# The first MLP's up-projection: 15 of its 22 pairs of output tiles by seven products instead of eight

## The chip, the cores and the metric

One core of one Trainium2 chip runs the whole program. The metric is the device time of one execution in microseconds (us); lower is better. TensorE (PE) does the matmuls, ScalarE (ACT), VectorE (DVE) and GpSimd (POOL) work on 128 x n tiles in SBUF and PSUM, and SyncE (SP) issues the DMA transfers. Each of these engines runs its own instructions strictly in the order of the program, and they wait for each other with counting semaphores.

## What is computed

Three layers on x of 512 rows (sequence) by 1024 columns in float32. The first layer has gated linear attention beside sliding-window attention, and then the gated MLP that the change is about; two more layers (dilated and differential attention, each with a squared-relu MLP) follow.

```python
h2 = rms_norm(x, ffn_norm)                       # 512 x 1024
u = causal_dwconv(h2 @ w_up, conv_w, conv_b)     # w_up 1024 x 5632, 3 taps along the sequence
a, bval = jnp.split(u, 2, axis=-1)               # 2 x 2816 columns
x = x + (jax.nn.silu(a) * bval) @ w_down         # w_down 2816 x 1024
```

## The kernel before

Everything is kept transposed: 128 features on the partitions, the 512 positions of the sequence along the free axis. Each float32 operand is split into a high part, rounded to `fp32r`, and a low part, the rest; a product is high x high + high x low + low x high, accumulated in PSUM.

**The up-projection.** w_up has 44 tiles of 128 output columns. They are taken in 22 pairs, one tile of `a` and the tile of `bval` that it gates; pair i gives block i of the gated result. `up_tile` is one tile: 8 blocks of the inner dimension, 24 matmuls of 512 columns (lines 1033, 1034, 1038), so a pair is 48. The weights come from HBM into the two halves of `stage`; ACT rounds a tile to `w_hi` (`split_hi`, line 1506), POOL makes `w_lo` in four pieces of 256 columns (`split_lo`, line 507). Four PSUM banks (`UP`) hold two pairs.

**Behind a tile** stands a fixed sequence: DVE scales the bank by `rstd` (line 2445), ACT begins the convolution (line 1767), DVE adds the other two taps (lines 2447 and 2450). Behind a pair: ACT silu (line 1770), DVE multiplies the halves (line 2455), ACT rounds the block to `f1_hi` (line 1772), DVE makes `f1_lo` (line 2458). All this is a hardware loop that does two pairs in one pass.

**The down-projection** follows: for each of the 8 output tiles, 22 blocks f times three matmuls of 512 columns (lines 1080, 1081, 1086). The order of all work is written out by hand for each engine.

**Seven products** are used already in the down-projections of the two later MLPs (`product`, lines 1425 to 1455, `fast_down`). The 2 x 2 block product of weights A and activations B is done in the Winograd form, with 7 products of half size: A11, S1, A12, S2, S4, S3, A22, where S1 to S4 are sums of blocks of A. A product is 12 matmuls of 256 columns (lines 1444, 1445, 1453). A group of four weight blocks is a quad; `slot_hi` and `slot_lo` hold its split blocks, `SUM_X` and `SUM_Y` are PSUM banks in which sums are made. In those MLPs DVE adds each product straight into x in SBUF (line 2890).

## Time and profile before

| | |
|---|---|
| device time, median of 3 runs | 1718.95 us (1718.62 to 1719.03) |
| the profiled execution | 1718.6 us, of which the span of the core's work is 1716.8 us |
| TensorE's granted clock | 0.999 of 2.4 GHz |
| busy: PE, DVE, ACT, POOL | 99%, 62%, 51%, 56% of the span |
| instructions in the trace | 27243, of which 9425 matmuls |

The profile is of one execution; times of single instructions and gaps come from it. Busy shares are averages over stages with different limits.

### The profile page before, as it was taken

The page shows a single profiled execution, that of the slowest core. Times are in us where ns is not written, and L with a number is a line of the kernel's source. Part 1 is how long each engine was busy: PE and PEld are TensorE (multiplying, and loading weights), DVE is VectorE, ACT ScalarE, POOL GpSimd, SP SyncE. Part 2 cuts the span into 40 slices and gives each one's busy share as a digit, 9 for nine tenths or more (in the row PEclk, how much of TensorE's full clock was granted, in tenths as well). Part 3 has the DMA queues.
Part 4 walks back from the last instruction along what each step waited for, and adds up shares of the span by engine and source line. Part 5 has one row for each costly group of instructions (what it writes and reads, how often), then busy time and mean ns, then how long its engine had stood idle before and what let it go on. Part 6 is the DMA issues. An engine that isn't in the chain of part 4 may idle for free.

```text
span 1716.8 us, 27243 instructions
## 1 busy us (share of the span) xinstructions
PE 1704.7 (99%) x9425; PEld 1440.6 (84%) x9425; DVE 1061.0 (62%) x2084; ACT 868.3 (51%) x1498; POOL 963.1 (56%) x1095
## 2 busy tenths in 40 slices
PE   9999999999999999999999999999999999999998
PEld 7778888888888778888989898977777889898988
DVE  6875755555311455568757575867776676757576
ACT  5665555555322444435545444546655554545355
POOL 5543655555555434357666666755554665656666
PEclk9999999999999999999999999999999999999999
DMA  5221333332334322223323323233322242333332
GB/s 192 74 68 61 100 98 98 97 93 93 108 95 137 104 68 83 74 74 123 99 98 99 105 96 106 64 128 116 105 97 70 87 133 91 109 99 98 99 98 74
DMA packets 48662, 167.91 MB, mean 98 GB/s; under 512 B 5376, under 2 KB 6672, under 8 KB 48528
## 3 DMA queue, kind: packets, MB, share of 16 engines
q1 hardware_dynamic: 48272, 166.05, 30.2%
q8 instruction: 61, 1.00, 0.2%
q10 hardware_dynamic: 288, 0.52, 0.1%
q14 instruction: 41, 0.34, 0.1%
HBM read 164.31 MB, written 2.24 MB: 97 GB/s over the span
## 4 chain that ended last, share of the span: by engine, by line
PE 90%; DVE 6%; ACT 2%; issue 1%; DMA 0%; POOL 0%; SPq 0%; DVEq 0%; ACTq 0%
PE bank L736 18%; PE bank L1444 6%; PE bank L1453 6%; PE bank L1445 6%; PE bank L661 5%; PE bank L660 5%; PE bank L666 5%; PE bank L1033 5%; PE bank L1034 5%; PE bank L1038 5%; PE bank L754 3%; PE bank L760 3%; PE bank L755 3%; PE bank L1086 2%; PE bank L1081 2%; PE bank L1080 2%
## 5 line engine op out<-in xcount | busy, mean ns | idle before, releaser
L507 POOL TENSOR_TENSOR w_lo<-stage,w_hi 128x256 fp32r<-128x256 f32 x872 | 672.2, 803 | 571.7 <-ACT w_hi L1506 317.5
L1506 ACT ACTIVATE w_hi<-stage 128x1024 fp32r<-128x1024 f32 x218 | 229.4, 1052 | 200.9 <-PE bank L1081 54.7
L660 PE MATMUL bank<-xn_hi,w_hi 128*128 128x512 f32 x544 | 211.8, 389 | 0.0
L661 PE MATMUL bank<-xn_lo,w_hi 128*128 128x512 f32 x544 | 211.7, 389 | 0.0
L736 PE MATMUL bank<-xn_hi,w_hi 128*128 128x512 f32 x464 | 189.1, 407 | 0.0
L736 PE MATMUL bank<-xn_lo,w_hi 128*128 128x512 f32 x464 | 181.8, 392 | 0.0
L2890 DVE TENSOR_TENSOR x<-x,bank 128x256 f32<-128x256 f32 (+1 forms) x217 | 97.4, 455 | 89.3 <-PE bank L1453 86.6
L1453 PE MATMUL bank<-arena 128*128 128x256 f32 x896 | 146.6, 283 | 0.0
L1033 PE MATMUL bank<-xn_hi,w_hi 128*128 128x512 f32 x352 | 137.1, 389 | 0.0
L1034 PE MATMUL bank<-xn_lo,w_hi 128*128 128x512 f32 x352 | 136.9, 389 | 0.0
L666 PE MATMUL bank<-xn_hi,w_lo 128*128 128x512 f32 x544 | 135.0, 389 | 0.0
L1444 PE MATMUL bank<-arena 128*128 128x256 f32 x512 | 129.4, 284 | 1.3 <-DVE arena L2910 0.8
L1445 PE MATMUL bank<-arena 128*128 128x256 f32 x512 | 128.7, 283 | 0.0
L1453 PEld LDWEIGHTS bank<-arena 128*128 128x128 f32 x896 | 124.8, 192 | 0.0
L736 PE MATMUL bank<-xn_hi,w_lo 128*128 128x512 f32 x464 | 123.9, 399 | 0.0
L666 PEld LDWEIGHTS bank<-xn_hi,w_lo 128*128 128x128 f32 x544 | 102.1, 188 | 21.2
L661 PEld LDWEIGHTS bank<-xn_lo,w_hi 128*128 128x128 f32 x544 | 102.2, 188 | 21.1
L660 PEld LDWEIGHTS bank<-xn_hi,w_hi 128*128 128x128 f32 x544 | 102.1, 188 | 20.9
L2910 DVE TENSOR_TENSOR arena<-tmp,arena 128x256 fp32r<-128x256 f32 (+2 forms) x128 | 115.0, 917 | 3.8 <-ACT arena L2067 2.5
L736 PEld LDWEIGHTS bank<-xn_hi,w_hi 128*128 128x128 f32 x464 | 87.2, 188 | 25.2 <-issue 8.5
L736 PEld LDWEIGHTS bank<-xn_hi,w_lo 128*128 128x128 f32 x464 | 84.6, 188 | 22.8 <-issue 6.0
L736 PEld LDWEIGHTS bank<-xn_lo,w_hi 128*128 128x128 f32 x464 | 87.3, 188 | 16.0
(374 smaller groups left out, 3719.3 us busy)
## 6 DMA issues: line engine op xcount, KB each, us to landing
stage<-weights SPq DMA_DIRECT2D x219, 512.0 KB, 3.6
prob<-pairs SPq DMA_DIRECT2D x32, 512.0 KB, 3.6
stage<-pairs SPq DMA_DIRECT2D x32, 512.0 KB, 3.6
bias<-table SPq DMA_DIRECT2D x11, 896.0 KB, 6.4
out<-y SPq DMA_DIRECT2D x8, 256.0 KB, 2.2
x<-x_in SPq DMA_DIRECT2D x3, 512.0 KB, 7.6
bias<-swa_table SPq DMA_DIRECT2D x4, 256.0 KB, 4.4
con<-consts SPq DMA_DIRECT2D x1, 640.0 KB, 9.8
```

The costliest lines, as they stand in the source:

```text
L507: ins = nc.gpsimd.tensor_tensor(w_lo[:, p_, ks], stage[:, p_, ks], w_hi[:, p_, ks].bitcast(F32), ALU.subtract)
L660: pe.matmul(G[p_][:], w_hi[:, p_, k], hi[:, k], start=(first and k == ks[0]), stop=False)
L661: mm = pe.matmul(G[p_][:], w_hi[:, p_, k], lo[:, k], start=False, stop=False)
L666: mm = pe.matmul(G[p_][:], w_lo[:, p_, k], hi[:, k], start=False, stop=(last and k == ks[-1]))
L736: mm = pe.matmul(G[p_][:], (w_hi if i < 2 * KD else w_lo)[:, p_, k], (xn_lo if i < 2 * KD and i % 2 else xn_hi)[:, k], start=(i == 0), sto ...
L1033: pe.matmul(UP[bank][:], w_hi[:, p_, k], xn_hi[:, k], start=(k == 0), stop=False)
L1034: mm = pe.matmul(UP[bank][:], w_hi[:, p_, k], xn_lo[:, k], start=False, stop=False)
L1444: pe.matmul(region, w, fc_hi[:, i, f], start=(fresh and i == 0), stop=False, skip_group_check=True)
L1445: pe.matmul(region, w, fc_lo[:, i, f], start=False, stop=False, skip_group_check=True)
L1453: mm = pe.matmul(region, w, fc_hi[:, i, f], start=False, stop=(i == QUADS - 1), skip_group_check=True)
L1506: act.activation(w_hi[:, p_], stage[:, p_], ACT.Copy).then_inc(hi_ready, 1)
L2910: dve.tensor_tensor(fc_lo[:, i, a:b + 1].rearrange("p c s -> p (c s)"), src, fc_hi[:, i, a:b + 1].rearrange("p c s -> p (c s)").bitcast(F3 ...
```

## The change

The up-projection takes 7 pairs as before (`N_PLAIN`) and the other 15 (`Q_UP`) by seven products. The four blocks of a quad are now the two tiles of a pair, each cut in the two halves of the inner dimension; the factors of B are the two halves of the normalized x by the two halves of the sequence.

- **Factors of B.** During plain pairs 0 to 3 DVE, ACT and POOL make the seven factors, high and low, from x and `rstd` (`factors_first`, `factors_second`, `factor_highs`, `factor_lows`). They lie in the upper part of `arena`.
- **Weights.** A quad comes from HBM as two transfers of 512 KB, two quads ahead. ACT copies one block to PSUM (`up_copy`), DVE makes the four sums (`up_sum`), ACT rounds seven blocks (`up_high`), DVE makes two of the low parts (`up_sum_low`) and POOL five (`up_low`).
- **Results.** They can't be added into an SBUF accumulator, since the convolution needs the product of the pair alone. Of the four quarters, C_00 is P1 + P2 and so on: ACT copies the partial products P1, U2 and U3 to SBUF and P5 to the pair's bank (`p1_copied`, `u2_copied`, `u3_copied`, `p5_copied`), and DVE adds (`c_00`, `c_01`, and two adds in `c_1`). There is no scaling by `rstd` for these pairs: it is in the factors.
- **Gating.** POOL now multiplies silu(a) by bval (`f_made_of`), for all pairs. The rounding (`f_high`) and the low parts (`f_low`) are done later: blocks 0 to 7 during quads 4 to 12, into the weight buffers `w_hi` and `w_lo` that are not used there; blocks 8 to 21 at the end of the last quad and behind it.
- **Down.** The first four down tiles are split on the way from the last quad (`down_split_hi`, `down_split_lo`) into slots that come free. Output tile 0 takes all its low parts of f last.
- **No loops.** The hardware loop of the up-projection is written out in line on all engines; the order on ACT and DVE where the plain pairs end is its own.

The diff, cut to its core:

```diff
-N_UP1 = 2 * NF1
+N_PLAIN = 7
+FACTORS_AT = [0, 1, 2, 3]
+Q_UP = NF1 - N_PLAIN
+N_UP1 = 2 * N_PLAIN
+UP_ORDER = [HI_A11, HI_S1, HI_A12, HI_S2, HI_S4, HI_A22, HI_S3]
+N_EARLY = 8
+EARLY_AT = 4
...
         def _(sp):
+            def up_load(q):
+                if q == 1:
+                    sp.wait_ge(lo_ready, T_DOWN1)
+                elif q >= 2:
+                    sp.wait_ge(slot_low, UP_LOW_AT[HI_A22, q - 2])
...
+            sp.wait_ge(slot_low, UP_LOW_AT[HI_A22, Q_UP - 1 - (Q_UP % 2)])
+            loads(T_DOWN1, T_QKV[0])
...
         def _(pool):
+            for q in range(Q_UP):
+                up_low(HI_S3, q)
+                if q == 0:
+                    up_low(HI_A22, 0)
+                if q + 1 < Q_UP:
+                    up_low(HI_A11, q + 1)
+                f_made_of(N_PLAIN + q - 1)
+                if q + 1 < Q_UP:
+                    for k in (HI_A12, HI_S4, HI_A22):
+                        up_low(k, q + 1)
+            for s_ in range(3):
+                down_split_lo(T_DOWN1 + s_)
+            f_made_of(NF1 - 1)
...
         def _(pe):
+            def up_product(q, k):
+                region = R2 if k in (HI_A12, HI_A22) else R5 if k in (HI_S1, HI_S4) else R1[q % 2][:, 0:HS]
...
+                elif k == HI_S2:
+                    pe.wait_ge(up_moved, moved_at(q, P1_COPY))
+                elif k == HI_S4:
+                    pe.wait_ge(up_moved, moved_at(q, P5_COPY))
+                elif k == HI_A22:
+                    pe.wait_ge(product_added, 4 * q + C_00)
+                elif k == HI_S3:
+                    pe.wait_ge(up_moved, moved_at(q, U2_COPY))
+                for i in range(QUADS):
+                    w, cols = up_hi[k][:, i * P:(i + 1) * P], slice(i * HS, (i + 1) * HS)
+                    pe.matmul(region, w, factor[:, f, 0, cols], start=(fresh and i == 0), stop=False, skip_group_check=True)
+                    pe.matmul(region, w, factor[:, f, 1, cols], start=False, stop=False, skip_group_check=True)
...
+                        if d == 0:
+                            pe.wait_ge(ffh_ready, FFH_PREP + f + 1)
...
         def _(act):
+            def p5_copied(q):
+                act.wait_ge(product_done, N_PROD * q + UP_AT[HI_S1])
+                act.wait_ge(conv_2, 2 * (N_PLAIN + q))
...
+            def up_copy(q):
+                act.wait_ge(quad_full[q % 2], 32 * (q // 2 + 1))
+                if q:
+                    act.wait_ge(sum_made, N_SUM * q)
+                act.activation(SUM_X[:], up_raw(q, 1)[:, 0:S], ACT.Copy).then_inc(slot_high, 1)
...
+            down_split_hi(T_DOWN1 + 2)
+            u3_copied(Q_UP - 1)
+            f_high(12)
+            conv_0_of(NF1 - 1, 1)
+            f_high(13)
+            silu(NF1 - 1)
+            for f in range(14, NF1 - 1):
+                f_high(f)
+            down_split_hi(T_DOWN1 + 3)
+            f_high(NF1 - 1)
...
         def _(dve):
+            up_sum_low(0, HI_S1)
+            scaled(N_PLAIN - 1, 1)
+            conv(N_PLAIN - 2, 1)
+            up_sum_low(0, HI_S2)
+            conv(N_PLAIN - 1, 0)
+            for q in range(Q_UP):
+                i, more = N_PLAIN + q, q + 1 < Q_UP
+                if q:
+                    c_1(q - 1)
+                else:
+                    conv(i - 1, 1)
+                if more:
+                    up_sum(q + 1, HI_S1)
+                    up_sum(q + 1, HI_S3)
+                    up_sum(q + 1, HI_S2)
+                if q:
+                    conv(i - 1, 1)
+                c_00(q)
+                if more:
+                    up_sum(q + 1, HI_S4)
+                    up_sum_low(q + 1, HI_S1)
+                    up_sum_low(q + 1, HI_S2)
+                c_01(q)
...
+                conv(i, 0)
+                if EARLY_AT < q <= EARLY_AT + N_EARLY:
+                    f_low(q - EARLY_AT - 1)
```

**DVE between two pairs.** Before, this is the loop's second pair (bank3 is the tile of bval, bank2 that of a):

```order
L2445 TENSOR_TENSOR bank3<-bank3,rstd 128x512
L2446 REGISTER_ALU
L2447 ISA
L2447 SCALAR_TENSOR_TENSOR tmp<-bank3,par,tmp 128x511
L2450 ISA
L2450 SCALAR_TENSOR_TENSOR tmp<-bank3,par,tmp 128x510
L2453 REGISTER_ALU
L2455 TENSOR_TENSOR bank2<-bank2,tmp 128x512
L2458 ISA
L2458 TENSOR_TENSOR arena<-bank2,arena 128x512
L2438 REGISTER_ALU
L2438 COMPARE_AND_BRANCH
```

After, this is one quad q from 5 to 12, from its second sum to its last instruction (`f_low`, line 2931); ahead of it stand the two adds of `c_1` on bank1 (lines 2923 and 2924) and the first sum (line 2882):

```order
L2886 TENSOR_TENSOR xn_raw<-stage,bank5 128x512
L2889 TENSOR_TENSOR bank5<-bank6,stage 128x512
L2832 SCALAR_TENSOR_TENSOR tmp<-bank1,par,tmp 128x511
L2835 SCALAR_TENSOR_TENSOR tmp<-bank1,par,tmp 128x510
L2910 TENSOR_TENSOR bank0<-rstd,bank4 128x256
L2894 TENSOR_TENSOR xn_raw<-stage,bank5 128x512
L2900 TENSOR_TENSOR v_split<-bank6,v_split 128x512
L2900 TENSOR_TENSOR bias_slots<-bank5,bias_slots 128x512
L2916 TENSOR_TENSOR bank0<-rstd,bank7 128x256
L2832 SCALAR_TENSOR_TENSOR tmp<-bank0,par,tmp 128x511
L2835 SCALAR_TENSOR_TENSOR tmp<-bank0,par,tmp 128x510
L2931 TENSOR_TENSOR arena<-arena_raw,w_hi 128x512
```

Eight arithmetic instructions for a pair have become fourteen, fifteen with `f_low`; the convolution (lines 2832, 2835) now has sums, adds and low parts ahead of it and between its halves, and the loop's register instructions are gone.

**ACT between two pairs.** Before, the second pair of a pass; line 1767 is the start of the convolution, 1770 silu, 1772 the rounding of the gated block:

```order
L1764 REGISTER_ALU
L1767 ISA
L1767 ACTIVATE tmp<-bank2,par 128x512
L1770 ACTIVATE bank2<-tmp 128x512
L1506 ACTIVATE w_hi<-stage 128x1024
L1764 REGISTER_ALU
L1767 ISA
L1767 ACTIVATE tmp<-bank3,par 128x512
L1771 REGISTER_ALU
L1772 ISA
L1772 ACTIVATE arena<-bank2 128x512
L1759 REGISTER_ALU
```

After, quad 4 from the second convolution of the pair before (line 2005 on bank1) on, with its copies of P5 (line 2051) and U2 (line 2057), the highs (line 2039), the copy to PSUM (line 2026) and the rounding of block 0 (line 2072, into w_hi):

```order
L2005 ACTIVATE tmp<-bank1,par 128x512
L2039 ACTIVATE v_split<-stage 128x512
L2051 ACTIVATE bank1<-bank7 128x256
L2039 ACTIVATE v_split<-bank6 128x512
L2039 ACTIVATE bias_slots<-stage 128x512
L2057 ACTIVATE rstd<-bank2 128x256
L2039 ACTIVATE bias_slots<-bank5 128x512
L2039 ACTIVATE bias_slots<-xn_raw 128x512
L2005 ACTIVATE tmp<-bank0,par 128x512
L2039 ACTIVATE xn_hi<-stage 128x512
L2026 ACTIVATE bank5<-xn_raw 128x512
L2072 ACTIVATE w_hi<-arena_raw 128x512
```

Two roundings of 1024 columns have become seven of 512 for a pair, and four copies of 256 and one of 512 are new; the copy of P5 now stands behind the start of the convolution of the pair before (line 2005).

**ACT where the up-projection ends.** Before, from the rounding of a pair's gated block, the loop's last instruction, on:

```order
L1772 ACTIVATE arena<-bank 128x512
L1759 REGISTER_ALU
L1759 COMPARE_AND_BRANCH
L1546 ACT_TABLE_LOAD
L1506 ACTIVATE w_hi<-stage 128x1024 x2
L1782 ACTIVATE xn_hi<-x,par 128x512
L1783 ACTIVATE tmp<-x 128x512
L1506 ACTIVATE w_hi<-stage 128x1024 x3
```

After, behind the last U2 copy: the start of the last pair's first convolution, then down tile 2 (line 2081 into v_split), the U3 copy (line 2063), the end of the last pair's convolution (line 2005) and silu (line 2011), and the roundings of blocks 11 to 21 (line 2072):

```order
L2005 ACTIVATE tmp<-bank,par 128x512
L2072 ACTIVATE arena<-arena_raw 128x512
L2081 ACTIVATE v_split<-stage 128x1024
L2063 ACTIVATE xn_raw<-bank 128x256
L2072 ACTIVATE arena<-arena_raw 128x512
L2005 ACTIVATE tmp<-bank,par 128x512
L2072 ACTIVATE arena<-arena_raw 128x512
L2011 ACTIVATE tmp<-tmp 128x512
L2072 ACTIVATE arena<-arena_raw 128x512 x2
L2072 ACTIVATE arena<-xn_raw 128x512 x5
L2081 ACTIVATE bias_slots<-stage 128x1024
L2072 ACTIVATE arena<-xn_raw 128x512
```

One rounding of a gated block ahead of the down-projection has become eleven, and ten of them stand behind a split that waits for a transfer.

## Rows read from the trace of the kernel before

**Rows 1.** The page: clock granted to TensorE in the 40 slices

```profile
PEclk9999999999999999999999999999999999999999
```

**Rows 2.** Waits of PE, whole run: us in total, times, longest

```profile
PE bank L920 <- DVE arena L2175: 1.5, 1, 1.5
```

**Rows 3.** Chain that ended last, 180 to 600: start us, us, what

```profile
431.54 1.81 PE bank L1038 x8
436.98 1.81 PE bank L1038 x8
442.42 1.81 PE bank L1086 x8
```

**Rows 4.** Timeline of PE, 844 to 848: start us, us, what, count

```profile
844.32 0.64 PE L1453 MATMUL bank<-arena 128*128 128x256 f32 x4
...
844.80 0.28 PE L1444 MATMUL bank<-arena 128*128 128x256 f32 x1
...
846.24 0.28 PE L1444 MATMUL bank<-arena 128*128 128x256 f32 x1
```

**Rows 5.** Timeline of ACT, 838 to 846; idle before in brackets

```profile
837.87 0.63 ACT L2031 ACTIVATE arena<-stage 128x512 fp32r<-128x512 f32 x1
...
838.39 0.60 ACT L2020 ACTIVATE bank<-prob 128x512 f32<-128x512 f32 x1
...
842.47 0.60 ACT L2031 ACTIVATE v_split<-bank 128x512 fp32r<-128x512 f32 x1 [2.60 <-DVE bank L2837]
...
842.96 0.62 ACT L2031 ACTIVATE v_split<-prob 128x512 fp32r<-128x512 f32 x1
...
845.06 0.63 ACT L2031 ACTIVATE arena<-v_tok 128x512 fp32r<-128x512 f32 x1 [0.84 <-PE bank L1453]
```

**Rows 6.** Timeline of DVE, 840 to 846

```profile
841.02 0.68 DVE L2834 TENSOR_TENSOR qkv<-prob,bank 128x512 f32<-128x512 f32 x1
841.73 0.70 DVE L2837 TENSOR_TENSOR bank<-bank,prob 128x512 f32<-128x512 f32 x1
842.34 0.41 DVE L2890 TENSOR_TENSOR x<-x,bank 128x256 f32<-128x256 f32 x1
842.67 0.68 DVE L2842 TENSOR_TENSOR v_tok<-prob,bank 128x512 f32<-128x512 f32 x1
843.27 0.68 DVE L2848 TENSOR_TENSOR arena<-bank,v_split 128x512 fp32r<-128x512 f32 x1
```

**Rows 7.** Timeline 300 to 325 of ACT, DVE and POOL, first MLP

```profile
304.03 0.78 ACT L1767 ACTIVATE tmp<-bank,par 128x512 f32<-128x512 f32 x1 [0.71 <-DVE bank L2445]
...
304.96 0.75 DVE L2447 SCALAR_TENSOR_TENSOR tmp<-bank,par,tmp 128x511 f32<-128x511 f32 x1 [1.10 <-ACT tmp L1767]
...
305.85 0.75 DVE L2450 SCALAR_TENSOR_TENSOR tmp<-bank,par,tmp 128x510 f32<-128x510 f32 x1
...
314.56 1.06 ACT L1506 ACTIVATE w_hi<-stage 128x1024 fp32r<-128x1024 f32 x1
...
315.53 0.76 ACT L1767 ACTIVATE tmp<-bank,par 128x512 f32<-128x512 f32 x1
...
315.78 2.83 POOL L507 TENSOR_TENSOR w_lo<-stage,w_hi 128x256 fp32r<-128x256 f32 x4 [4.57 <-ACT w_hi L1506]
```

**Rows 8.** Groups by form, whole run: count | busy us, mean ns | idle before

```profile
L549 POOL TENSOR_TENSOR arena<-stage,arena 128x512 fp32r<-128x512 f32 x16 | 20.8, 1298 | 0.5
...
L2910 DVE TENSOR_TENSOR arena<-tmp,arena 128x512 fp32r<-128x512 f32 x32 | 30.5, 953 | 0.0
...
L2059 ACT ACTIVATE arena<-tmp 128x256 fp32r<-128x256 f32 x32 | 13.4, 418 | 1.0
```

**Rows 9.** Timeline 831.7 to 832.9: PE resumes behind DVE

```profile
831.75 0.96 DVE L2910 TENSOR_TENSOR arena<-tmp,arena 128x768 fp32r<-128x768 f32 x1
...
832.85 0.36 PE L1444 MATMUL bank<-arena 128*128 128x256 f32 x1 [0.29 <-DVE arena L2910]
```

**Rows 10.** The page: DMA issues, KB each, median us to landing

```profile
stage<-weights SPq DMA_DIRECT2D x219, 512.0 KB, 3.6
```

More of the change, by code:

```diff
@@ L151, in program @@
             pass
+        with nc.sbuf_tensor("xn_raw", [P, 2 * KD, S], F32) as xn_raw:
+            pass
         xn_hi = sb("xn_hi", [P, KD, S], F32R)
@@ new lines, in program, with up_raw, up_s3 @@
+        up_slots += [xn_hi[:, 0], xn_hi[:, 1]]
+        up_hi = {k: up_slots[2 * i] for i, k in enumerate(SLOT_ORDER)}
+        up_lo = {k: up_slots[2 * i + 1] for i, k in enumerate(SLOT_ORDER)}
+        def up_raw(q, r):
+            if q % 2:
+                return stage[:, r].rearrange("p k c -> p (k c)")
+            blocks = xn_raw[:, KD + 2 * r:KD + 2 * r + 2] if q else arena_raw[:, 12 + 2 * r:14 + 2 * r]
+            return blocks.rearrange("p k s -> p (k s)")
+        def up_s3(q):
+            return xn_raw[:, 3 - q % 2] if q else arena_raw[:, 10]
@@ L210, in program @@
         MB = banks[7]
-        UP = banks[0:4]
         END_MEAN = (MB, OB)
@@ new lines, in f_made_of, with f_low, down_low @@
+            def f_made_of(i):
+                pool.wait_ge(silu_done, i + 1)
+                pool.wait_ge(conv_2, 2 * i + 2)
+                nc.gpsimd.tensor_tensor(f1[i], conv_acc(i, 0), conv_acc(i, 1), ALU.mult).then_inc(f_made, 1)
+            def f_low(f):
+                pool.wait_ge(ffh_ready, FFH_PREP + f + 1)
+                nc.gpsimd.tensor_tensor(f1_lo[f], f1[f], f1_hi[f].bitcast(F32), ALU.subtract).then_inc(factor_low, 1)
+            def down_low(t):
+                for k in range(0, KD, KD // 4):
+                    ks = slice(k, k + KD // 4)
+                    ins = nc.gpsimd.tensor_tensor(down_lo(t)[:, ks], stage[:, t % 2, ks], down_hi(t)[:, ks].bitcast(F32), ALU.subtract)
+                ins.then_inc(lo_ready, 1)
@@ new lines, in _ @@
+            for s_ in range(3):
+                down_split_lo(T_DOWN1 + s_)
+            f_made_of(NF1 - 1)
+            for f in POOL_LOWS:
+                f_low(f)
+            down_split_lo(T_DOWN1 + 3)
+            with pool.Fori((T_DOWN1 + 4) // 2, T_QKV[0] // 2) as m:
+                for p_ in range(2):
+                    pool.wait_ge(hi_ready, 2 * m + p_ + 1)
+                    pool.wait_ge(tile_done, 2 * m + p_ - 1)
+                    down_low(T_DOWN1 + 4 + p_)
+            split_los(T_QKV[0], T_MLP2[0])
@@ new lines, in _ @@
+            split_hi(T_MLP1 // 2 + 1, 0)
+            for i in range(N_PLAIN - 1):
+                conv_0_of(i, 0)
+                split_hi(T_MLP1 // 2 + i + 1, 1)
+                if i == N_PLAIN - 2:
+                    act.wait_ge(tables_saved, 80)
+                    up_copy(0)
+                silu(i)
+                conv_0_of(i, 1)
+                if i < N_PLAIN - 2:
+                    split_hi(T_MLP1 // 2 + i + 2, 0)
+                if i in FACTORS_AT:
+                    factor_highs(FACTORS_AT.index(i))
@@ new lines, in _ @@
+            act.wait_ge(ff_ready, FF_PREP)
+            act.wait_ge(factor_low, QUADS)
+            up_high(HI_A11, 0)
+            up_high(HI_S1, 0)
+            up_high(HI_A12, 0)
+            conv_0_of(N_PLAIN - 1, 0)
+            up_high(HI_S2, 0)
+            up_high(HI_S4, 0)
+            up_copy(1)
+            for q in range(Q_UP):
+                i, more = N_PLAIN + q, q + 1 < Q_UP
+                if q == 0:
+                    p1_copied(0)
+                    conv_0_of(i - 1, 1)
+                    up_high(HI_S3, 0)
+                    silu(i - 1)
+                    up_high(HI_A22, 0)
+                else:
+                    u3_copied(q - 1)
+                    silu(i - 1)
+                    up_high(HI_S3, q)
+                    p1_copied(q)
+                    if not more:
+                        down_split_hi(T_DOWN1)
+                    conv_0_of(i - 1, 1)
+                if more:
+                    up_high(HI_A11, q + 1)
+                p5_copied(q)
+                if more:
+                    up_high(HI_S1, q + 1)
+                    up_high(HI_A12, q + 1)
+                else:
+                    down_split_hi(T_DOWN1 + 1)
+                    for f in range(N_EARLY, 11):
+                        f_high(f)
+                u2_copied(q)
+                if more:
+                    up_high(HI_S2, q + 1)
+                    up_high(HI_S4, q + 1)
+                conv_0_of(i, 0)
+                if more:
+                    up_high(HI_A22, q + 1)
+                else:
+                    f_high(11)
+                if q + 2 < Q_UP:
+                    up_copy(q + 2)
+                if EARLY_AT <= q < EARLY_AT + N_EARLY:
+                    f_high(q - EARLY_AT)
@@ new lines, in f_low @@
+            def f_low(f):
+                dve.wait_ge(ffh_ready, FFH_PREP + f + 1)
+                if f >= N_IN_ARENA:
+                    dve.wait_ge(product_done, N_PROD * Q_UP)
+                dve.tensor_tensor(f1_lo[f], f1[f], f1_hi[f].bitcast(F32), ALU.subtract).then_inc(ff_ready, 1)
+            for i in range(N_PLAIN - 1):
+                scaled(i, 0)
+                conv(i, 0)
+                if i - 1 in FACTORS_AT:
+                    factor_lows(FACTORS_AT.index(i - 1))
+                if i in FACTORS_AT:
+                    factors_first(FACTORS_AT.index(i))
+                scaled(i, 1)
+                if i < N_PLAIN - 2:
+                    conv(i, 1)
+                if i in FACTORS_AT:
+                    factors_second(FACTORS_AT.index(i))
@@ L2461, in _ @@
+            c_1(Q_UP - 1)
+            f_low(10)
+            conv(NF1 - 1, 1)
+            for f in DVE_LOWS:
+                if f > 10:
+                    f_low(f)
+            dve.wait_ge(f_made, NF1)
             dve.memset(acc, 0.0).then_inc(acc_zero, 1)
```

472 lines of the change are left out of this document (362 added, 110 removed).

## Prediction

> **What bounds the kernel now.** I read the clock first, then PE's waits, then the chain of work that ended last, then the timelines of the places the change touches. TensorE has its full clock, 2.4 GHz, in every slice [rows 1]. Its longest wait in the whole run is 1.5 us, and not in the first MLP [rows 2]. In the chain a tile of the up-projection starts 5.44 us after the one before, and the first down tile as long after the last up tile [rows 3]: the stage is PE's stream and nothing else, 5.44 / 24 = 0.227 us for a matmul of 512 columns, 10.88 us for a pair. So a pair is worth what its matmuls take, as long as the other engines keep up; and where they don't, the wait is new.
>
> **What is removed.** A quad has 7 x 12 = 84 matmuls of 256 columns. In the later MLPs a product takes 846.24 - 844.80 = 1.44 us, 0.12 for a matmul [rows 4], so a quad is 10.08 us. That is 0.80 us less than a pair now, for 15 pairs **12.0 us**. (Half the columns cost more than half the time, 0.120 against 0.227; with exactly half it would be 20 us.) Nothing else leaves PE's stream; down, 528 matmuls, stays.
>
> **What is added, per quad.** The prices are the distances from start to start, since the next instruction starts before the last one ends. DVE [rows 6]: 0.61 for 512 columns with one operand in PSUM, 0.33 for 256 (taken as 0.34), 0.71 where it waits for its own predecessor. ACT: 0.52 for 512 from SBUF (837.87 to 838.39), 0.49 from PSUM (842.47 to 842.96) [rows 5]. ACT's 256 from PSUM isn't in the rows: 0.418 us for 256 from SBUF [rows 8] against 0.63 for 512 is 0.21 less, so I take 0.28 to the next start and 0.39 to its end, the 512 from PSUM less that difference. Bounds: 0.25 (half of 0.49) and 0.42; two of them are in the round below. The start of a convolution is 0.78 long, the next two steps 0.75 each [rows 7]. POOL's 512 is 1.30 [rows 8]; six make 7.8 us, so POOL isn't near the limit.
> DVE in sum: four adds 1.36, four sums 2.5, two lows 1.2, two convolutions 2.9: 8.0 us of 10.08. ACT: seven highs and a copy to PSUM 4.1, four copies 1.1, two starts 1.35, silu 0.52: 7.1 us. Neither is full. But they hand work to each other, each in fixed order, and the round of these handovers is the thing to time.
>
> **The round of DVE and ACT.** Count from the first add of `c_1`. Two adds 0.68, three sums 1.93, the convolution 0.78 + 0.75 and a handover of 0.04: 4.18. Then `p5_copied` 0.28, S1 and A12 high 1.01, `u2_copied` 0.28, S2 high 0.63: 6.38. DVE's low of S2 0.61, `c_01` 0.47, ACT's start of the next convolution 0.81, DVE's two steps 0.78 + 0.67: **9.72 us**, 0.36 less than PE's 10.08. The handovers are those of the later MLPs, 0.04 (DVE at 842.43 to ACT at 842.47 [rows 5, 6]).
> In PE's time: the U3 copy starts 0.26 after the last product's end (845.06 against 844.80 [rows 4, 5]), so `c_1` at 0.69, and P5 is copied at 0.69 + 4.18 + 0.39 = 5.26. Product S4 is the fifth and wants its region at 5.76. PE needs 0.14 from DVE's end (832.71) to its own start, and loses 0.07 on the first matmul (0.36 instead of 0.28) [rows 9], so the margin is 0.29 us. This is the place where PE waits first. C_00 (5.1 against 7.2) and U2 (6.5 against 8.6) have more.
>
> **Quads 5 to 12** also have `f_low` at the end of the round, with both inputs in SBUF. Such a DVE instruction of 512 columns takes 953 ns in the mean where POOL works beside it [rows 8] against 0.68 for one with PSUM, and POOL is then in its low of A22. I take 0.95, to the next start 0.87: the round is 10.59, 0.51 over PE's. Eight times 0.51 less the margin is **3.8 us**. Bounds: alone it would be 0.61 (10.33, 1.7 us in all); behind the 0.5 us that is left of a POOL instruction 1.11 (10.83, 5.7 us). ACT's `f_high` fits.
> The Trainium skill, "SBUF — State Buffer", section "SBUF: two separate sides", says that DVE with two SBUF inputs and GpSimd exclude each other for a whole instruction. The rows agree in direction, 953 ns instead of 0.68 us. By that rule `f_low` would wait about 0.39 for the low of A22 and then take 0.69, and the sum would be some 1.0 us higher.
>
> **Where the plain pairs end** DVE is behind, since the banks of pair 6 are read only once its matmuls are done. From the start of quad 0: `scaled` to 0.81, convolution of pair 5 to 2.26, low of S2 ends 2.95; only then may ACT copy for quad 1 (`up_copy` waits for that low), then P1 (due 4.32, there at 3.9), and start the convolution of tile 13 at 3.76. DVE: tile 12 to 4.32, tile 13 from 4.57 to 6.10. ACT is then in A11 high until 6.50, P5 is copied at 6.89, S4 starts at 7.10 instead of 5.76. C_00 stands behind three sums and ends at 8.37; A22 starts at 8.58 and quad 1 at 11.46, **1.38 us** late. In quad 1 the round is still 1.18 late and margin 0.29: **0.89**. Quads 2 to 4 make it up at 0.36 each. Together 2.3 us; bounds 1.4 (quad 1 unhindered) and 3.5.
>
> **Where the quads end.** The down-projection's tile 0 needs the 22 highs in turn; block 21 is wanted behind 21 high and 16 low matmuls, 37 x 0.227 = 8.4 us after the last product. ACT comes to it late. In quad 14 a split of 0.97 stands ahead of the convolution of pair 20, which starts at 2.95 and ends at 5.3; POOL's multiplication (1.30) waits for it, so its low parts of down tile 0 run from 6.6 to 9.45 (2.83 for four pieces [rows 7]). Only then may tile 2 be loaded into the same half of `stage`; 3.6 us [rows 10] to 13.1, that is 3.0 after the last product. ACT waits for it ahead of the U3 copy. Then tile 2's split 0.97 (1.06 long, 314.56 to 315.53 [rows 7]), U3 0.28, block 12, `c_1` on DVE until 5.3, the convolution's start, block 13, silu 7.0, seven blocks 10.7, tile 3's split 11.6, block 21 at 12.3. PE restarts at 12.46 instead of 8.39: **4.1 us**. Bounds: 2.5 if the transfer takes 2 us or POOL is earlier, 5 if POOL is held up by DVE's low parts.
>
> **Moved at no cost.** The factors: in pairs 0 to 3 DVE keeps four convolution steps (3.0) and two scalings (1.4) and gets about 6 us of factors (eight instructions, by 0.34 to 0.95 each); POOL has two tiles' low parts, 5.7, plus 1.30 and, for 1024 columns of factors, 2.6. Both near 10; the cover is two pairs of PSUM banks (PE needs a bank a whole pair later), and if it failed the price would be some 0.5 us a pair, 2 us. A quad's transfers: issued 0.8 us into quad q - 2, two times 3.6 in a row end at 8.0, `up_copy` wants them at 9.4. SP has nothing else queued there.
>
> **Sum.** -12.0 + 2.3 + 3.8 + 4.1 = -1.8 us on the profiled 1718.6, which is 0.35 below the median of 1718.95. Prediction 1717.2 us.
>
> **Rivals.**
> 1. *The handovers cost what they cost in the present loop.* There ACT's end at 304.81 to DVE's start is 0.15, and a convolution step 0.89 instead of 0.78 [rows 7]. Four handovers 0.12 dearer and two steps 0.11 dearer make the round 10.42, 11.29 with `f_low`. Then quads with and without it lose 1.21 and 0.34 each: 8 x 1.21 + 6 x 0.34 = 11.7 in place of 3.8, and 0.4 more at the start: 6.5 us slower, 1725.5. For it: the same instructions. Against it: in the loop a register instruction stands ahead of each wait, and none does after. It decides the sign from 0.15 us a quad in the round on. Chance 0.18; with other new waits on this side (late POOL lows, factors) 0.23.
> 2. *Better cover.* `f_low` finds POOL idle (1.7) and the end costs 2.5: -5.5, 1713.4. Chance 0.32; the bounds of all terms together give -12.0 + 1.4 + 1.7 + 2.5 = -6.4, 1712.5.
> 3. *Full gain*, if the round is nowhere late and ACT not at the end: 1707. Against it: the end needs only rows that are there. Chance 0.02.
> Forecast as worked out, 1715.5 to 1722: 0.43.
>
> **How the numbers follow.** 0.2%, 3.4 us, is about what a measurement of this kernel can tell from no change. Faster takes rivals 2 and 3, 0.34; slower 0.22; same 0.44. The range 1711.5 to 1725 reaches past rival 2 with all its bounds and to rival 1; the dearer bound of the two copies, 0.28 in the round, is 2.2 us over quads 5 to 12 and inside it. The likeliest one's own is 1715 to 1721.
>
> **What would show it.** Product starts 1.44 apart in the quads; quad 0 about 11.5 us and quad 1 about 11.0, with PE waiting for the P5 copy (line 2051) and C_00 (line 2910); quads 2 to 4 at 10.08; quads 5 to 12 near 10.6, waiting for the P5 copy; PE waiting for line 2072 or ACT for the transfer of a down tile, some 4 us, in the first down tile; `f_low` near 0.95 us. It is wrong if a quad without `f_low` takes over 10.1, if waits show in the plain pairs, if the granted clock falls below 2.4 GHz where PE idles, or if down tile 2 is there in time.

## The result and the profile after

The changed kernel takes 1724.04 us in the median of 9 runs (1723.23 to 1724.91), the kernel before 1718.9 (1718.56 to 1719.03): a ratio of 1.003 [1.002, 1.004], 5.1 us slower. The number lies in the predicted range of 1711.5 to 1725, but the forecast was 1717.2 us and "same", so it has the sign wrong (-1.8 us forecast, +5.1 measured). The profiled executions differ by as much: spans of 1721.9 and 1716.8 us.

To see where that is, PE's stream in the first MLP is cut into three parts by the starts of its first matmuls. The first is the 14 tiles of the plain pairs, which before go at 7.01, 5.58 and then 5.44 us. The second is 15 quads, which took 15 x 10.88 = 163.2 us as pairs. The third is the first down tile of 66 matmuls, 66 x 0.227 = 14.96 us. Starts one after the other in the trace after, in us:

```
plain tiles  7.02 5.57 5.44 5.44 5.44 5.44 5.44 6.98 5.58 8.71 6.34 5.91 5.45 5.44
quads        11.51 11.15 10.08 10.08 10.08 10.08 10.34 10.59 10.59 10.60 10.58 10.61 10.58 10.58 10.33   (sum 157.78)
down tile 0  19.08
```

| part | predicted | measured |
|---|---|---|
| plain pairs | 0 | +6.3 |
| quads: matmuls saved | -12.0 | -12.0 |
| quads 0 and 1 late | +2.3 | +2.5 |
| quads made late by `f_low` | +3.8 | +4.1 |
| down tile 0 | +4.1 | +4.1 |
| sum | -1.8 | +5.0 |

Four of the five terms came out within 0.3 us of what was worked out. The one that was put at nothing cost 6.3 us.

The waits of PE after (us in total, times, longest), to be read beside [rows 2]:

```profile
PE bank L1263 <- ACT bank L2051: 4.0, 9, 1.2
PE bank L1228 <- POOL w_lo L623: 2.0, 2, 1.8
PE bank L1308 <- ACT arena L2072: 1.6, 2, 1.1
...
PE bank L1223 <- ACT w_hi L1744: 1.4, 2, 1.0
```

The wait that was longest before is no longer among the first three. L1263 is a product of a quad waiting for a region that ACT copied, L1308 the down-projection waiting for gated blocks. Both were forecast. L1228 and L1223 belong to the plain pairs: PE there waits for the halves of the weights, from POOL and from ACT, which it never did before.

**The plain pairs.** PE's timeline after, tiles 9 and 10, counted from 0 (start us, us, what, idle before in brackets):

```profile
255.55 2.66 PE L1228 MATMUL bank<-xn_hi,w_lo 128*128 128x512 f32 x8 [1.81 <-POOL w_lo L623]
258.66 0.80 PE L1223 MATMUL bank<-xn_hi,w_hi 128*128 128x512 f32 x1 [0.45 <-ACT w_hi L1744]
```

PE's idle time is put down to POOL and ACT. But both are waiting themselves, each for the next: POOL for ACT's high half, ACT for DVE. The same time on POOL, ACT and DVE, from their timelines:

```profile
244.40 3.21 POOL L623 TENSOR_TENSOR w_lo<-stage,w_hi 128x256 fp32r<-128x256 f32 x4 [3.19 <-ACT w_hi L1744]
247.56 1.29 POOL L726 TENSOR_TENSOR arena_raw<-tmp 128x512 f32<-128x512 f32 x1
248.81 2.41 POOL L712 TENSOR_TENSOR arena<-arena_raw,arena 128x1024 fp32r<-128x1024 f32 x1
```

```profile
242.60 0.78 ACT L2005 ACTIVATE tmp<-bank,par 128x512 f32<-128x512 f32 x1 [5.88 <-DVE bank L2825]
243.28 1.04 ACT L1744 ACTIVATE w_hi<-stage 128x1024 fp32r<-128x1024 f32 x1
246.34 0.42 ACT L2017 ACTIVATE arena<-arena_raw 128x256 fp32r<-128x256 f32 x1 [2.02 <-DVE arena_raw L2862]
246.66 1.47 ACT L2018 ACTIVATE arena<-arena_raw 128x1536 fp32r<-128x1536 f32 x1
248.04 0.76 ACT L2005 ACTIVATE tmp<-bank,par 128x512 f32<-128x512 f32 x1
...
256.89 0.78 ACT L2005 ACTIVATE tmp<-bank,par 128x512 f32<-128x512 f32 x1 [5.86 <-DVE bank L2825]
```

```profile
237.10 1.22 DVE L2871 TENSOR_TENSOR arena<-v_tok,arena 128x512 fp32r<-128x512 f32 x1
238.25 1.22 DVE L2851 SCALAR_TENSOR_TENSOR arena_raw<-x,par,rstd 128x512 f32<-128x512 f32 x1
239.40 1.22 DVE L2853 SCALAR_TENSOR_TENSOR arena_raw<-x,par,rstd 128x512 f32<-128x512 f32 x1
...
241.87 0.70 DVE L2825 TENSOR_TENSOR bank<-bank,rstd 128x512 f32<-128x512 f32 x1
243.41 0.75 DVE L2832 SCALAR_TENSOR_TENSOR tmp<-bank,par,tmp 128x511 f32<-128x511 f32 x1 [0.85 <-ACT tmp L2005]
...
248.83 0.75 DVE L2832 SCALAR_TENSOR_TENSOR tmp<-bank,par,tmp 128x511 f32<-128x511 f32 x1 [1.92 <-ACT tmp L2005]
...
256.15 0.70 DVE L2825 TENSOR_TENSOR bank<-bank,rstd 128x512 f32<-128x512 f32 x1
```

From the scaling (L2825) of one pair's tile to the same of the next pair is 256.15 - 241.87 = 14.28 us, and ACT's convolution starts are as far apart (256.89 - 242.60 = 14.29). PE makes a pair in 10.88. So each pair with factors falls 3.4 us further behind. In the round DVE waits 0.85 + 1.92 = 2.8 us for ACT, and has some 11.5 us of work, in which every instruction of 512 columns with its inputs in SBUF takes 1.22 us. DVE's 0.85 is ACT's own start of the convolution, 0.78 long, with the handovers. The 1.92 is an order: ACT starts the pair's second convolution (248.04) only behind the factors' highs (246.34 and 246.66), and these wait for DVE. POOL stands idle for 3.19 us of the same round; the other 11.1 us it works, longer than PE's pair as well. Its four pieces from 251.18 take 4.3 us, where four such pieces take 2.83 in [rows 7]. Neither DVE nor ACT waits for POOL in this round: it is closed by DVE and ACT alone.

**The quads.** PE's timeline after, quad 7, where it waits for the copy of P5:

```profile
358.96 0.64 PE L1271 MATMUL bank<-arena,bias_slots 128*128 128x256 f32 x4
...
360.40 0.64 PE L1271 MATMUL bank<-arena,bias_slots 128*128 128x256 f32 x4
361.33 0.35 PE L1263 MATMUL bank<-arena,bias_slots 128*128 128x256 f32 x1 [0.30 <-ACT bank L2051]
```

Products are 360.40 - 358.96 = 1.44 us apart, as in [rows 4]. The next one, due at 360.88 (360.40 + 0.48 for the four matmuls), starts at 361.33, with a first matmul of 0.35 instead of 0.28, much as in [rows 9]. DVE's timeline has the cause: `f_low` (L2931) takes 0.96 us, 0.89 to the next start, at the end of the round that leads up to this copy.

```profile
355.74 0.96 DVE L2931 TENSOR_TENSOR arena<-arena_raw,w_hi 128x512 fp32r<-128x512 f32 x1
356.63 0.42 DVE L2923 TENSOR_TENSOR bank<-xn_raw,bank 128x256 f32<-128x256 f32 x1
```

**The end.** ACT's timeline after: the split of down tile 2 waits for its transfer, then the U3 copy, and the rounding of the last of the 22 gated blocks starts 11.0 us after the last product's end (439.58) and ends 11.6 us after it.

```profile
442.10 1.06 ACT L2081 ACTIVATE v_split<-stage 128x1024 fp32r<-128x1024 f32 x1 [2.47 <-DMA stage<-weights]
443.07 0.36 ACT L2063 ACTIVATE xn_raw<-bank 128x256 f32<-128x256 f32 x1
...
450.57 0.62 ACT L2072 ACTIVATE arena<-xn_raw 128x512 fp32r<-128x512 f32 x1
```

The chain that ended last after, where [rows 3] had 1.81 us for eight matmuls, and the windows over the down tile (length, then busy us and count of PE, PEld, DVE, ACT and POOL, the granted clock as a share of 2.4 GHz, DMA share, GB/s):

```profile
447.67 2.98 PE bank L1315 x8
```

```profile
440.00:447.00 7.00, 5.40 (x22) 3.75 (x21) 5.42 (x9) 4.59 (x8) 5.96 (x8) 1.00 0.43 148
447.00:451.00 4.00, 3.97 (x12) 3.03 (x12) 4.00 (x6) 4.00 (x8) 1.66 (x2) 0.63 0.39 131
```

PE's waits are 1.6 us of the 4.1. Behind them the granted clock was 0.63 over 4 us, that is, part of that stretch ran at the lower level of 1.2 GHz, and eight matmuls took 2.98 us there. As an estimate from that row, 4 x (1 - 0.63) = 1.5 us of the 4.1 is the clock's; the last 1 us stands in neither. [rows 1] had full clock in every slice; here the dip is too short to show in a slice of 43 us.

### The profile page after: what moved, and what is told of

Same layout as the page of the kernel before. It is cut to its first block, busy times and chain, and to the rows that moved or that the text cites. A ratio compares the mean times of both kernels' runs of the same rounds, so it can differ in the third digit from the quotient of the medians.

```text
span 1721.9 us, 28210 instructions
## 1 busy us (share of the span) xinstructions
PE 1699.8 (99%) x9965; PEld 1458.2 (85%) x9965; DVE 1136.7 (66%) x2214; ACT 898.7 (52%) x1635; POOL 1023.9 (59%) x1076
## 4 chain that ended last, share of the span: by engine, by line
PE 68%; DVE 4%; ACT 1%; issue 1%; POOL 0%; DMA 0%; DVEq 0%; ACTq 0%; SPq 0%; POOLq 0%
PE bank L923 14%; PE bank L1682 6%; PE bank L1691 6%; PE bank L1683 6%; PE bank L847 6%; PE bank L848 6%; PE bank L853 6%; PE bank L1315 2%; PE bank L1308 2%; PE bank L1310 2%; PE bank L941 2%; PE bank L947 2%; PE bank L942 2%; PE bank L1541 1%; PE bank L1570 1%; DVE arena L3435 1%
## 5 line engine op out<-in xcount | busy, mean ns | idle before, releaser
L623 POOL TENSOR_TENSOR w_lo<-stage,w_hi 128x256 fp32r<-128x256 f32 x664 | 531.6, 834 | 423.2 <-ACT w_hi L1744 221.3
L1744 ACT ACTIVATE w_hi<-stage 128x1024 fp32r<-128x1024 f32 x166 | 174.7, 1052 | 156.5 <-PE bank L923 51.8
L847 PE MATMUL bank<-xn_hi,w_hi 128*128 128x512 f32 x544 | 211.8, 389 | 0.0
L848 PE MATMUL bank<-xn_lo,w_hi 128*128 128x512 f32 x544 | 211.8, 389 | 0.0
L923 PE MATMUL bank<-xn_hi,w_hi 128*128 128x512 f32 x464 | 189.0, 407 | 0.0
L923 PE MATMUL bank<-xn_lo,w_hi 128*128 128x512 f32 x464 | 181.8, 392 | 0.0
L1691 PEld LDWEIGHTS bank<-arena 128*128 128x128 f32 x896 | 124.7, 192 | 0.0
L1682 PEld LDWEIGHTS bank<-arena 128*128 128x128 f32 x512 | 98.2, 192 | 2.6 <-issue 2.5
L1683 PEld LDWEIGHTS bank<-arena 128*128 128x128 f32 x512 | 98.2, 192 | 0.0
```

Source lines behind the costliest of these rows:

```text
L623: ins = nc.gpsimd.tensor_tensor(w_lo[:, p_, ks], stage[:, p_, ks], w_hi[:, p_, ks].bitcast(F32), ALU.subtract)
L847: pe.matmul(G[p_][:], w_hi[:, p_, k], hi[:, k], start=(first and k == ks[0]), stop=False)
L848: mm = pe.matmul(G[p_][:], w_hi[:, p_, k], lo[:, k], start=False, stop=False)
L923: mm = pe.matmul(G[p_][:], (w_hi if i < 2 * KD else w_lo)[:, p_, k], (xn_lo if i < 2 * KD and i % 2 else xn_hi)[:, k], start=(i == 0), sto ...
L1682: pe.matmul(region, w, fc_hi[:, i, f], start=(fresh and i == 0), stop=False, skip_group_check=True)
L1683: pe.matmul(region, w, fc_lo[:, i, f], start=False, stop=False, skip_group_check=True)
```

## Experiments

The theory, A: the plain pairs are late because a factor pair's round of DVE and ACT is longer than PE's pair. It is longer because DVE's SBUF instructions collide with POOL's (A1) and because of the waits between ACT and DVE (A2), and four such pairs in a row add up past what the buffers cover. Its rival, B: the transfer for quad 0, which stands between the tiles' loads, delays the weights. For the other two terms: C, `f_low` on DVE costs all 4 us in the quads; D, the late blocks at the end come from the order of POOL's low parts and ACT's split of down tile 3. The parts of each run's profiled execution, against the kernel before:

| kernel | median us (runs) | ratio to before | plain | quads | down tile 0 |
|---|---|---|---|---|---|
| after | 1724.04 (9) | 1.003 [1.002, 1.004] | +6.3 | -5.4 | +4.1 |
| e1_spread | 1719.7 (10) | 1.0006 [0.9996, 1.0016] | +2.0 | -5.1 | +5.2 |
| e2_act_order | 1725.5 (5) | 1.0038 [1.0024, 1.0052] | +7.3 | -5.5 | +4.2 |
| e3_load_late | 1725.02 (6) | 1.0033 [1.0021, 1.0046] | +6.3 | -5.4 | +6.3 |
| e4_pool_low | 1720.28 (10) | 1.0009 [0.9999, 1.0019] | +6.4 | -9.3 | +3.6 |
| e5_end_order | 1720.57 (10) | 1.0009 [1.0000, 1.0018] | +6.3 | -5.4 | +0.9 |
| e6_combined | 1712.96 (5) | 0.9965 [0.9952, 0.9979] | +2.0 | -9.4 | +0.7 |
| e7_few_pieces | 1718.51 (10) | 0.9997 [0.9988, 1.0006] | 0.0 | -5.2 | +4.1 |
| e8_pairs_0235 | 1712.39 (5) | 0.9963 [0.9949, 0.9976] | +1.4 | -8.5 | +1.1 |

The kernel before took 1718.95 us beside e1 to e4 and 1719.0 beside e5 to e8.

### e1_spread: a pair without factors between them

```diff
-FACTORS_AT = [0, 1, 2, 3]
+FACTORS_AT = [0, 1, 3, 4]
```

> The change with the factors of B made in plain pairs 0, 1, 3 and 4 instead of 0 to 3. Theory: in a pair with factors the hand-over between DVE and ACT goes round in 14.3 us (228.29 to 242.60 in the trace after) where PE needs 10.88, and the delay adds up over four pairs in a row; PE loses 6.3 us by it. With pair 2 free in between the delay peaks lower, and PE's waits in the plain pairs fall to 2 to 3 us: about 1720. Rival, transfers: PE's tiles are late because quad 0's transfer stands among the loads of the tiles; then nothing changes, 1724.

The plain pairs lost 2.0 us instead of 6.3, and the median fell by 4.3. The same factor instructions cost PE a third once one pair without them lies between. So the lateness adds up over neighbouring pairs, and it isn't the factors' sum over the stage that counts.

### e2_act_order: ACT's factor highs behind the next pair's first convolution

```diff
                 conv_0_of(i, 0)
+                if i - 1 in FACTORS_AT:
+                    factor_highs(FACTORS_AT.index(i - 1))
                 split_hi(T_MLP1 // 2 + i + 1, 1)
...
                     split_hi(T_MLP1 // 2 + i + 2, 0)
-                if i in FACTORS_AT:
-                    factor_highs(FACTORS_AT.index(i))
```

> The change with ACT rounding a pair's factors behind the start of the next convolution, not ahead of it. Theory (order): DVE's wait for ACT of 1.92 us a pair falls to 0.85, the round to about 13.2 us, and the delay after four pairs is 3 to 4 us less: about 1720.5. Rival (POOL is overloaded by 9.7 us a pair) and rival (transfers): no change, 1724.

The theory expected 1720.5 here, and the median is 1725.5, slower by 1.5 than the changed kernel. The wait it was made for did fall from 1.92 to 0.85 us, but the round got no shorter: from 242.29 to 256.90, 14.61 us where the changed kernel has 14.28. DVE's waits are 1.7 of it instead of 2.8, its work 12.9 instead of 11.5. The timeline of e2_act_order shows why:

```profile
248.18 0.75 DVE L2834 SCALAR_TENSOR_TENSOR tmp<-bank,par,tmp 128x511 f32<-128x511 f32 x1 [0.85 <-ACT tmp L2005]
...
249.91 2.40 POOL L712 TENSOR_TENSOR arena<-arena_raw,arena 128x1024 fp32r<-128x1024 f32 x1 [0.63 <-ACT arena L2018]
249.96 2.89 DVE L2873 TENSOR_TENSOR arena<-arena_raw,arena 128x512 fp32r<-128x512 f32 x1
```

The factors' low parts of DVE and POOL now start together, and DVE's 512 columns take 2.89 us where the same instruction took 1.22 (L2871 above): it ends 0.5 behind POOL's 1024 columns. So A2 is no cause that can be taken away by itself here. What the order gives back, the collision takes.

### e3_load_late: quad 0's transfer four tiles later

```diff
-            loads(T_MLP1 + 4, T_MLP1 + 8)
+            loads(T_MLP1 + 4, T_MLP1 + 12)
             up_load(0)
-            loads(T_MLP1 + 8, T_DOWN1)
+            loads(T_MLP1 + 12, T_DOWN1)
```

> The change with quad 0's two transfers issued four tiles later. Rival (transfers): PE's waits in the plain pairs get 2 us or more shorter, 1722 or less. Theory: no change, 1724.

The plain pairs lost 6.3 us as before. Rival B is refuted. The median rose by 1.0 and the profiled down tile by 2.2. That profile is of the slowest of the six runs, 1726.25 us; more on that tile below.

### e4_pool_low: f_low on POOL

```diff
-POOL_LOWS = []
+POOL_LOWS = list(range(8))
...
                     for k in (HI_A12, HI_S4, HI_A22):
                         up_low(k, q + 1)
+                        if k == HI_A12 and EARLY_AT < q <= EARLY_AT + N_EARLY:
+                            f_low(q - EARLY_AT - 1)
...
                 conv(i, 0)
-                if EARLY_AT < q <= EARLY_AT + N_EARLY:
-                    f_low(q - EARLY_AT - 1)
```

The second hunk is in POOL's loop over the quads, the last in DVE's.

> The change with the low parts of gated blocks 0 to 7 made by POOL in quads 5 to 12 instead of by DVE. Theory: the low part is what makes the round of DVE and ACT 10.6 us; without it the round is 9.7 and all quads from 2 to 13 run at PE's 10.08: 4.0 us less, 1720. Rival: POOL, with 9.1 us of work in a quad, becomes the late one, and the quads stay over 10.3: 1722 or more.

Quads 2 to 13 all take 10.08 us and quad 14 takes 10.19, and the sum of the quads is 3.9 less than after. The median fell by 3.8. Theory C holds, and the other half of it too: without `f_low` the round is short enough. POOL had the room.

### e5_end_order: down tile 0's low parts ahead, tile 3's split behind

```diff
                 if q + 1 < Q_UP:
                     up_low(HI_A11, q + 1)
+                else:
+                    down_split_lo(T_DOWN1)
                 f_made_of(N_PLAIN + q - 1)
...
-            for s_ in range(3):
+            for s_ in range(1, 3):
...
-            down_split_hi(T_DOWN1 + 3)
             f_high(NF1 - 1)
+            down_split_hi(T_DOWN1 + 3)
```

> The change with two moves at the end of the up-projection: POOL makes the low part of down tile 0 ahead of the multiplication for pair 20, so that tile 2 is loaded some 3.5 us earlier, and ACT rounds block 21 ahead of down tile 3. Theory: the first down tile waits for ACT, which waits for that load ahead of the last pair's U3 copy; it takes 19.2 us instead of 15.0 and the moves give back 3 us or more: 1721 or less. Rival: ACT's eleven roundings are themselves too many, and the gain is under 1 us.

The down tile took 15.8 us instead of 19.1, and the median fell by 3.5. ACT's timeline of e5_end_order has tile 2's split 2.5 us earlier (3.5 were expected) and without a wait:

```profile
439.57 1.05 ACT L2083 ACTIVATE v_split<-stage 128x1024 fp32r<-128x1024 f32 x1
440.52 0.37 ACT L2065 ACTIVATE xn_raw<-bank 128x256 f32<-128x256 f32 x1
```

The windows of the same kernel, read as those of after, have the clock at its full level throughout:

```profile
440.00:447.00 7.00, 6.83 (x29) 5.06 (x29) 6.93 (x10) 5.87 (x12) 4.89 (x5) 1.00 0.46 149
447.00:451.00 4.00, 4.00 (x19) 3.26 (x18) 4.00 (x7) 3.76 (x5) 1.44 (x2) 1.00 0.01 2
```

Theory D holds for the two moves together. The two edits were made together, so the share of each is open.

### e6_combined: e1, e4 and e5 together

> The change with factors in pairs 0, 1, 3, 4, POOL making the early low parts, and the end's two moves. The theory takes the three losses as separate: 1724.0 - 4.4 - 3.8 - 3 = 1712 to 1713. Rival (they cover each other, or POOL becomes late): 1716 or more.

The median is 1712.96 us, 0.35% and 6.0 us faster than the kernel before. In the profiled execution, 1712.06 us, the parts add up: +2.0 - 9.4 + 0.7 = -6.7, and its span is 6.6 shorter. The three gains of e1, e4 and e5 in the median, 4.3, 3.8 and 3.5, would give 1712.4, 0.5 less than the 1712.96. The five runs of e6_combined spread by 1.8 us, so no interaction of the three shows. Its waits of PE:

```profile
PE bank L1265 <- ACT bank L2053: 2.0, 2, 1.3
...
PE bank L1230 <- POOL w_lo L623: 0.9, 1, 0.9
```

The first is the start of the quads, the second the plain pairs; no wait of the down tile is left among them.

### e7_few_pieces: three of POOL's four pieces left out

It is made for A1, and it leaves work out: of the four pieces of each plain tile's low half POOL makes the first alone, three are not computed.

```diff
-            def split_lo(m, p_):
+            def split_lo(m, p_, pieces=4):
...
-                for k in range(0, KD, KD // 4):
+                for k in range(0, pieces * (KD // 4), KD // 4):
```

The two calls for the plain pairs pass `pieces=1`.

> The change with POOL making only the first of the four pieces of a tile's low part in the plain pairs, the other three left out (the output is then not the reference's). Theory, contention: a factor instruction of DVE with both inputs in SBUF takes 1.22 us instead of 0.7 because POOL is at work in SBUF at that time; with POOL mostly idle the instructions take about 0.7, the round of a factor pair falls from 14.3 to 11.5 us or less and PE's waits in the plain pairs from 6.3 to below 2: 1719 or less. Rival, order alone (DVE and ACT wait for each other): the instructions' lengths don't matter much, 1722 or more.

The plain pairs lost nothing, with the factors in pairs 0 to 3 and ACT's order as in the changed kernel. Some of DVE's groups by form from 208 to 276 us (count, busy us, mean ns, idle before), first of after, then of e7_few_pieces:

```profile
L2868 DVE TENSOR_TENSOR arena<-arena_raw,arena 128x256 fp32r<-128x256 f32 x2 | 3.1, 1572 | 0.0
L2851 DVE SCALAR_TENSOR_TENSOR v_tok<-x,par,rstd 128x512 f32<-128x512 f32 x2 | 2.4, 1221 | 0.0
L2871 DVE TENSOR_TENSOR arena<-v_tok,arena 128x512 fp32r<-128x512 f32 x2 | 2.4, 1221 | 0.0
...
L2862 DVE TENSOR_TENSOR v_tok<-v_tok 128x256 f32<-128x256 f32 x2 | 1.7, 842 | 0.1
L2855 DVE TENSOR_TENSOR v_tok<-v_tok 128x256 f32<-128x256 f32 x2 | 1.7, 838 | 0.1
```

```profile
L2871 DVE TENSOR_TENSOR arena<-v_tok,arena 128x512 fp32r<-128x512 f32 x2 | 2.5, 1227 | 0.0
L2862 DVE TENSOR_TENSOR v_tok<-v_tok 128x256 f32<-128x256 f32 x2 | 2.2, 1118 | 0.1
...
L2851 DVE SCALAR_TENSOR_TENSOR v_tok<-x,par,rstd 128x512 f32<-128x512 f32 x2 | 1.5, 742 | 0.0
...
L2868 DVE TENSOR_TENSOR arena<-arena_raw,arena 128x256 fp32r<-128x256 f32 x2 | 1.4, 695 | 0.0
...
L2855 DVE TENSOR_TENSOR v_tok<-v_tok 128x256 f32<-128x256 f32 x2 | 0.8, 424 | 0.1
```

Three of these five are shorter: 0.74 instead of 1.22, 0.70 instead of 1.57, 0.42 instead of 0.84. L2871 is as long as before and L2862 is longer, since POOL's gating (L726) and the pieces that are left still run beside them. So the round fell, but not to the 11.5 us or less that was expected. DVE's scaling of the second tile of a pair stands at these times:

```profile
236.30 0.70 DVE L2825 TENSOR_TENSOR bank<-bank,rstd 128x512 f32<-128x512 f32 x1
...
249.19 0.70 DVE L2825 TENSOR_TENSOR bank<-bank,rstd 128x512 f32<-128x512 f32 x1
```

That round is 12.9 us; the two ahead of it are 11.9 and 12.2 (from 212.24 and 224.10). All three are longer than PE's 10.88, together by 4.3 us, and PE lost nothing by it: the buffers covered it. In the changed kernel the same three rounds come to 11.0 us of lateness.

Shown is that with less work on POOL the whole loss of 6.3 us is gone, while DVE's waits for ACT, 0.85 and 1.92 in a round, are as they were. The round is closed by DVE and ACT: in the changed kernel POOL waits 3.19 us for ACT in each round and ACT 5.88 for DVE, while neither DVE nor ACT waits for POOL. What POOL does to that round it does by making DVE's instructions longer. But POOL's own way to the low halves, for which PE waited 2.0 us, got shorter in this run too. How much of the 6.3 us comes by each way is not shown.

### e8_pairs_0235: e6 with one more gap

As e6_combined, with `FACTORS_AT = [0, 2, 3, 5]`.

> As the combined kernel, with the factors in pairs 0, 2, 3 and 5. Theory: delays add up over two pairs at most and there is more room between, but the last factors end beside quad 0's sums; between 1711 and 1715, better than the combined one if its plain pairs still wait 1 us or more and quad 0 starts no later.

1712.39 us (1711.99 to 1713.57) against e6's 1712.96 (1712.05 to 1713.89): the two cannot be told apart. In the profiled executions the plain pairs gain 0.7 and quad 0 loses as much (12.39 instead of 11.69). In the kernel's order the last factors now come right before DVE's sums for quad 0; whether that is the cause was not tried.

## Why the prediction was wrong

**The failed step** is "Moved at no cost", on the factors: "Both near 10; the cover is two pairs of PSUM banks (PE needs a bank a whole pair later), and if it failed the price would be some 0.5 us a pair, 2 us." It added busy times of DVE and of POOL, each by itself, and compared each sum with 10.88. Three things were wrong in that.
- The durations. "eight instructions, by 0.34 to 0.95 each" has as its upper end the 0.95 us of a DVE instruction that runs beside POOL [rows 8]. In the round shown above six of the eight took 0.83 to 1.22 us, and the eight together 7.2 us instead of 6. DVE's work came to 11.5 us, not 10.4, and POOL's to 11.1, not 9.6. Just ahead of the first MLP the trace of before has such instructions beside the same pieces, and they would have given the right price. DVE's and POOL's timelines of before, 196 to 201 us:

```profile
199.26 1.23 DVE L2340 SCALAR_TENSOR_TENSOR xn_lo<-x,par,xn_hi 128x512 fp32r<-128x512 f32 x1
200.41 1.22 DVE L2337 TENSOR_TENSOR tmp<-tmp 128x512 f32<-128x512 f32 x1
```

```profile
198.05 3.03 POOL L507 TENSOR_TENSOR w_lo<-stage,w_hi 128x256 fp32r<-128x256 f32 x3 [1.12 <-ACT w_hi L1506]
```

- The waits. Here the round was never laid out step by step, as it was for the quads. It has 2.8 us in which DVE waits for ACT. 11.5 and 2.8 make the 14.3 us that the trace shows, 3.4 a pair over PE's 10.88, and not 0.5.
- The cover. It was counted as if it renewed itself, and by the wrong buffer. Over three rounds the same scaling goes from 212.52 to 256.15 us, 43.6 where PE needs 32.6; of these 11.0 us PE lost 6.3, so 4.7 were covered, once. e7_few_pieces, 4.3 us late over three rounds, lost nothing, and e1_spread, with one free pair between, lost 2.0. What ran out was not the PSUM banks but the weights: PE's waits are for `w_lo` and `w_hi`. In ACT's order the rounding for a tile stands behind the start of the convolution of the third tile before it. So tile 10 starts at 258.66 us, when ACT has begun tile 7's convolution at 256.89 and then rounded tile 10's half; tile 10's bank had been free since the convolution of tile 6 ended, at 250.37.

The prediction named "waits ... in the plain pairs" among what would make it wrong, and rival 1 included "factors" with the 0.05 it gave to other waits on the slower side. That chance was too small: rows of a collision of DVE and POOL were at hand, and the one that was used, the 0.95, was right for `f_low` and too low here.

**What is removed** was right: 1.44 us a product and 10.08 a quad wherever nothing else is late.

**Where the plain pairs end**: 1.38 and 0.89 predicted, 1.43 and 1.07 measured, in quads 0 and 1, with PE waiting for the copy of P5 (L2051). In quad 0 it waits 1.18 us there, ahead of the fifth product, as forecast.

**Quads 5 to 12**: 10.59 predicted for a round with `f_low`, 10.59 measured, but in quads 7 to 13. An `f_low` at the end of a quad delays the copy of P5 in the next, and the margin takes up part of the first one, so quad 6 has 10.34. That makes 3.8, as forecast. The other 0.25 of the 4.1 is quad 14. There the split of down tile 0 (L2081, at 431.31) stands ahead of the convolution's start that the copy of P5 has to wait for, and e4_pool_low, without `f_low` on DVE, still loses 0.11 in that quad; the prediction had this split, but charged it to the end alone. e4_pool_low confirms the cause and the 9.72 us round below it, in so far as that lies under 10.08. Rival 1, handovers as dear as in the present loop, is refuted by the same 10.08 us quads: it would have made them 10.42.

The rule weighed in the prediction, the Trainium skill, "SBUF — State Buffer", section "SBUF: two separate sides", has DVE with two SBUF inputs and GpSimd exclude each other for a whole instruction. For `f_low` the row was the better guide to the size: 0.96 us, where the working by the rule had 0.39 + 0.69. In the plain pairs the rule comes nearer than the 0.95. Of e2_act_order's 2.89 us, 2.35 are the rest of POOL's instruction and 0.54 come behind it, somewhat less than the 0.68 that L2871 takes by itself in e7_few_pieces (220.79 us); no row shown of before has such a pair of instructions.

**Where the quads end**: 4.1 predicted and measured, but partly by another road. The last block was rounded 11.6 us after the last product, not 12.3. PE's waits were 1.6 us and the clock fell behind them. Where it did not, in e4_pool_low, a like lateness has 2.2 us of waits and costs 3.6; the 1.4 between are not shown as waits. So at full clock the term is 3.6, and the size was right by some luck: the mechanism (ACT behind tile 2's load) was right, as e5_end_order shows, and a falling clock was named only as something that would make the forecast wrong.

**Left open.** The last 2 us of the plain pairs and the 2.5 at the start of the quads are still there in e6_combined. e8_pairs_0235 takes 0.7 from the first and adds more to the second (3.5); nothing else was tried. Why e3_load_late made the down tile 2.2 us longer than the changed kernel isn't settled. It has 2.5 us of waits instead of 1.6 there, and the granted clock was 0.52 over 4 us and 0.83 over the 8.6 behind them, instead of 0.63 and 0.97. By the estimate used above that is 3.4 us of clock instead of 1.7, which is enough for the difference. But no instruction there was moved, e1_spread has the same 2.5 us of waits with a clock of 0.65, and each run has one profile.

## What to carry to other kernels

When work is moved onto engines that are "not full", lay their round out instruction by instruction with its waits, as far as the bound engine's period, in every stage it touches, not only in the one that looks tight; two sums of busy time that both fit prove nothing. Price an SBUF-to-SBUF instruction of DVE by the row nearest to what GpSimd does at that moment, and look first whether the move can be spread: here the buffers covered 4.7 us of lateness, about one late round, and a free round between late ones gave the cover back. Count that cover by the buffer that runs out first, along each engine's order. A wait of TensorE can cost more than the list of waits shows: 2.2 us of them went with 3.6 at full clock (e4_pool_low), 1.6 with 4.1 where the clock fell. So an end where buffers arrive late is worth an edit of its own.
